# A sixth feature-major product pair and a new order of ScalarE's and VectorE's steps in a two-block sequence model

## What is computed

```python
    x = x + (p[i] @ ple_w[i]) * gate
    return rmsnorm(x, norm_final)
...
    h = rms_norm(x, norm_g[l])
    proj = jnp.einsum('bsd,de->bse', h, w_in[l])
    (a_q, a_k, a_v, a_z, m_q, m_k, m_v, m_o, m_z, m_i, m_f,
     c_a, c_b, c_z) = split_columns(proj)
    ...
    qk = jax.nn.silu(causal_depthwise_conv(jnp.concatenate([m_q, m_k], axis=-1), ...))
    ...
    u = c_a * jax.nn.sigmoid(c_b)
    u = causal_depthwise_conv(u, cv_dw_w[l], cv_dw_b[l])      # 31 taps
```

## Time and profile before

| | us |
|---|---|
| median of 3 runs (3367.03 to 3368.46) | 3367.67 |
| the profiled execution, its own time | 3364.18 |
| its span, first to last instruction | 3362.6 |
| PE busy | 3231.2 (96%) |
| DVE busy | 1950.9 (58%) |
| POOL busy | 1706.8 (51%) |
| ACT busy | 1240.3 (37%) |

### The profile page before, as it was taken

The page is one execution under the profiler, slowest core; times in us unless marked ns, Lnnn a source line. Parts: engine busy times, 40 slices in busy tenths (PEclk is TensorE's granted clock), DMA queues, the critical chain, the costliest instruction groups (busy, mean ns, idle before and its releaser), DMA issues. The chain is left out here.

```text
span 3362.6 us, 43705 instructions
## 1 busy us (share of the span) xinstructions
PE 3231.2 (96%) x16157; PEld 2632.0 (78%) x16157; DVE 1950.9 (58%) x2345; ACT 1240.3 (37%) x1871; POOL 1706.8 (51%) x1142
## 2 busy tenths in 40 slices
PE   5989999999999999999999999999999999898999
PEld 5767878888888778888878888888777788577887
DVE  8687355555555766793456555555758678355511
ACT  5323353333333443312343333333444312566511
POOL 5812856666666326542865556666523742244521
PEclk9999999999999999999999999999999999999999
DMA  6364111111111213323311111111212232425653
GB/s 233 115 132 133 51 52 56 50 50 50 54 52 50 94 44 125 119 101 134 113 60 48 53 50 50 50 54 52 94 48 103 94 122 99 178 79 181 209 149 105
DMA packets 156942, 309.90 MB, mean 92 GB/s; under 512 B 16752, under 2 KB 92016, under 8 KB 154112
## 3 DMA queue, kind: packets, MB, share of 16 engines
q1 hardware_dynamic: 140640, 265.88, 24.4%
q10 hardware_dynamic: 16160, 42.08, 3.3%
HBM read 234.98 MB, written 72.94 MB: 92 GB/s over the span
## 5 line engine op out<-in xcount | busy, mean ns | idle before, releaser
L2137 PE MATMUL ps_job<-AHL,WH 128*128 128x512 f32 x3072 | 951.6, 391 | 16.6 <-POOL WL L1531 10.0
L1531 POOL TENSOR_TENSOR WL<-WR,WH 128x1024 fp32r<-128x1024 f32 x170 | 427.0, 2512 | 770.8 <-ACT WH L1123 769.1
L2137 PEld LDWEIGHTS ps_job<-AHL,WH 128*128 128x128 f32 x3072 | 578.7, 189 | 141.2 <-POOL WL L1531 14.1
L2137 PE MATMUL ps_job<-AHL,WL 128*128 128x512 f32 x1536 | 599.8, 391 | 0.0
L1123 ACT CAST WH<-WR 128x1024 fp32r<-128x1024 f32 x214 | 225.0, 1052 | 752.7 <-PE ps_job L2137 509.3
L2137 PEld LDWEIGHTS ps_job<-AHL,WL 128*128 128x128 f32 x1536 | 289.8, 189 | 60.5
L1833 DVE SCALAR_TENSOR_TENSOR ps_job<-ps_job,RB 128x1024 f32<-128x1024 f32 (+1 forms) x80 | 79.9, 1017 | 405.6 <-PE ps_job L2137 396.1
L1592 POOL TENSOR_TENSOR OPS_L<-VS,OPS_H 128x1024 fp32r<-128x1024 f32 (+2 forms) x96 | 193.5, 2030 | 55.9 <-ACT OPS_H L1312 51.3
L2286 PE MATMUL ps_job<-OPS_H,WH 128*128 128x512 f32 x512 | 199.5, 390 | 0.7 <-POOL WL L1531 0.7
L2286 PE MATMUL ps_job<-OPS_L,WH 128*128 128x512 f32 x512 | 199.3, 389 | 0.0
L2286 PE MATMUL ps_job<-OPS_H,WL 128*128 128x512 f32 x512 | 199.3, 389 | 0.0
(11 more groups left out here) (535 smaller groups left out, 7209.3 us busy)
## 6 DMA issues: line engine op xcount, KB each, us to landing
WR<-in_wall SPq DMA_DIRECT2D x244, 512.0 KB, 3.3
fm_scratch<-VS ACTq DMA_DIRECT2D x32, 512.0 KB, 3.1
tm_scratch<-VS ACTq DMA_DIRECT2D x24, 512.0 KB, 2.7
s_Win<-in_x_chunk SPq DMA_DIRECT2D x8, 1024.0 KB, 7.9
s_U<-in_x_group SPq DMA_DIRECT2D x8, 1024.0 KB, 12.4
s_mt<-z_scratch SPq DMA_DIRECT2D x64, 128.0 KB, 4.6
prod_scratch<-s_Win SPq DMA_DIRECT2D x16, 512.0 KB, 2.6
X<-in_x_feat SPq DMA_DIRECT2D x2, 4096.0 KB, 15.8
```

Of the source, the lines that this page charges most:

```text
L1531: pool.tensor_tensor(dst, raw, src.bitcast(F32), ALU.subtract).then_inc(raw_free, 1)
L2137: last = pe.matmul(out, l, r, start=(k == 0 and i == 0), stop=(k == k_tiles - 1 and i == 2))
```

## The change

The pairs begin at j = 6, so that projections 6 and 7 (kind silu) become a pair as well. ScalarE, not VectorE, makes the scaled YR, after its activation of j == 1. VectorE makes the four sums at j == 1, ahead of the final rows. The casts and low parts of T move to j == 2 and 3. `third_sum` goes into the eviction of the odd job, ahead of its last tap or ahead of the plain eviction. The taps' counts after each j change.

```diff
-PAIRED_FM = range(8, 18, 2)
+PAIRED_FM = range(6, 18, 2)
...
-TAPS_AT = {j: 3 for j in range(18, 20)} | {j: 5 for j in range(20, 32)}
+TAPS_AT = {j: 3 for j in range(18, 20)} | {j: 2 for j in range(20, 24)} | {j: 4 for j in range(24, 28)} | {j: 8 for j in range(28, 32)}
...
                     take(j)
+                    if j == 1:
+                        act.wait_ge(xadd, N_XADD * tb + (2 + N_XADD))
+                        for k in range(KD):
+                            act.activation(YR[:, k], X[:, k], ACT.Copy, scale=gains[:, GAIN_OF[2], k:k + 1]).then_inc(f_raw, 1)
                     if j in (1, 2):
                         store_rows(j - 1)
-                    if j in (3, 4):
-                        t_high((range(KD // 2), range(KD // 2, KD))[j - 3], 1)
+                    if j in (2, 3):
+                        t_high((range(KD // 2), range(KD // 2, KD))[j - 2], 1)
...
+                def put(j):
+                    if KINDS[j] == "silu":
+                        take(j)
+                    store(j)
...
-                        store(j - 2)
+                        put(j - 2)
...
-                    store(j - 1)
+                    if i:
+                        put(j - 1)
+                    else:
+                        store(j - 1)
...
-                def convolve(j, i):
+                def convolve(j, i, between=None):
...
                         if k:
                             step(ins)
+                        if k == 1 and between:
+                            between()
...
-                def evict(j):
+                def evict(j, between=None):
                     if KINDS[j] == "conv":
-                        convolve(j, j - M_QK.start)
+                        convolve(j, j - M_QK.start, between)
                     else:
+                        if between:
+                            between()
                         slot_free(j)
-                        dve.tensor_tensor(V[j % 2][:], ps4[slot_of(j)][:], halves(RB[:]), ALU.mult).then_inc(copied, 1)
+                        done = scaled if KINDS[j] == "silu" else copied
+                        dve.tensor_tensor(V[j % 2][:], ps4[slot_of(j)][:], halves(RB[:]), ALU.mult).then_inc(done, 1)
...
                     if i:
-                        evict(j - 1)
-                    third_sum(n, FM, slots[1])
+                        evict(j - 1, lambda: third_sum(n, FM, slots[1]))
+                    else:
+                        third_sum(n, FM, slots[1])
...
                     if j == 1:
-                        for k in range(KD):
-                            dve.tensor_scalar(YR[:, k], X[:, k], gains[:, GAIN_OF[2], k:k + 1], None, ALU.mult).then_inc(f_raw, 1)
-                        final_rows()
-                    if j == 2:
                         dve.wait_ge(f_raw, KD * (tb + 1))
                         t_sums(1)
+                        final_rows()
                     if j == 3:
                         dve.wait_ge(st_x[1], 16 * tb + 16)
-                    if j == 4:
+                    if j == 3:
                         t_low(1)
```

## The result

| | us |
|---|---|
| after, median of 4 runs (3414.24 to 3418.81) | 3414.82 |
| before, same session, median of 4 runs (3365.11 to 3368.46) | 3367.35 |
| ratio, 95% interval | 1.0145, 1.0132 to 1.0159 |
| the profiled execution of after, its own time | 3415.3 |
| its span (before: 3362.6) | 3413.4 |

The change makes the kernel 1.4% slower. 3413.9 was forecast. The spans differ by 50.8 us, the medians by 47.5; the profiled execution of before was a quick one (3364.18 against a median of 3367.67), so the sum of 46.2 has to answer for 50.8, not for 47.5. About 3 us of the closeness of the forecast is luck.

What follows compares the result with a forecast made beforehand. TensorE, busy 96% of the span, was taken as the bound. Forecast: 40.0 us more at the fronts, less 5.5, 3.9 and 3.9, plus 19.5 for the tail: 46.2 more, 3367.7 + 46.2 = 3413.9 us; range 3392 to 3427.

Steps and rivals of the forecast that it cites:

- The queue at the front: ScalarE, each block: the first rows' store waits for the third final row, delaying tile 4's cast from 1263.06 to 1275.3.
- Tile 4's low part: GpSimd's subtraction ahead of job 4: shut out by VectorE's final rows, 7.7 us, ending at 1284.1 instead of 1271.9.
- the first wait: TensorE ahead of job 4 in each block: waits 10.8 us for GpSimd's subtraction of tile 4.
- a train with gaps: Rival: GpSimd gets in between final rows; eighth row and job 5 2.3 us later; 4.6 more, 3418.5; chance 0.15.
- Job 5: TensorE, each block: tile 5 stands behind T's low parts on GpSimd; starts at 1303.1, 18.9 us lost.
- The restart: TensorE runs at a lower granted clock after a long wait: 1.6 us lost, charged once a block.
- The tail: VectorE, block 1: 36 taps behind j = 27 take 51.8 us; TensorE waits 17.9 us inside j = 31.
- The small waits: Four TensorE waits on `third_sum` in block 1 and four at the gates in both blocks go: 3.9 us less each.

Runs made afterwards that it cites:

- b4: The kernel before, with VectorE waiting for its own last scaled row between the scalings and the final rows; 3364.77 us in one run.
- b1: The kernel before with only the change's new taps' counts added; 3381.88 us, ratio 1.0052 to before.
- a1: The kernel after with the taps' counts of before put back; 3400.06 us, ratio 1.0103 to before.
- b2: The kernel before with only `third_sum` put ahead of the last convolution step; 3359.67 us, ratio 0.9988 to before.
- the early stop: The kernel before, with VectorE waiting for its own scaled rows behind the fourth scaling instead of the eighth; 3366.63 us in one run.
- c1: The kernel after with stores behind the T_H casts, tile 5 ahead of T's low parts on GpSimd, and 21 taps behind j = 27; 3388.51 us, ratio 1.0063 to before.

## Why the prediction was right

**The queue at the front: right.** The store of the first rows went to stand behind the sums and final rows and held the cast of tile 4 back: forecast 1275.3, measured 1275.66. The run with the store moved shows that it is this.

**Tile 4's low part: wrong, and the sum hardly felt it.** The step "the overlap is now almost the same, so everything moves by the 12.2 us of the final rows", with 7.7 us for the subtraction, failed. The trace of after has 2.92, and the first wait is 5.76 us instead of 10.8. I took the 7.70 of before as what such a meeting costs. The same meeting in the kernel before costs 2.97 when VectorE pauses for 0.1 us ahead of the final rows (b4); in after, four sums that wait for one another stood ahead of them. The Trainium skill (SBUF — State Buffer, section SBUF: two separate sides: the shared pair of ports is held for the whole instruction, the other engine blocks until then) gave the right answer for after (2.92) and for the run with the stop (2.97). The train of before does not agree with it: GpSimd stood through the rest of a row, three more rows and a c_a step (7.70). The rival "a train with gaps" named what followed: the eighth row 2.1 us later (11.73 against 9.64), and job 5 with it.

**Job 5: right in mechanism, 1.4 us too small.** Predicted 18.9 us late, measured 1305.10 - (1251.95 + 3 x 10.94) = 20.3. The rival had 21.2. Five GpSimd steps and VectorE's four between them took 15.56 us, 16.0 were charged; they began at 1289.49 instead of 1287.1, of which 0.56 is the whole block's (its j = 2 began at 1251.95, not 1251.39) and the rest goes with the 2.1 above. The moved tile 5, with 12.6 us less in the fronts, shows that it was this order on GpSimd that cost.

**The restart: mis-sized.** 1.6 us were charged. Job 5 lost 12.59 - 10.94 = 1.65, right. In j = 31 it was more: from the use of the scans' sixth step to the next step of the same job (`m_ends`) are 8.7 us in after (2889.59 to 2898.28) and 5.9 in before (2845.04 to 2850.92), so 2.8. Behind the same wait b1 lost 2.2 and the run with tile 5 first 1.5, so one number doesn't fit them all. Job 4 lost 2.50, hidden behind job 5's wait, as said.

**The tail: right.** 51.8 us were charged for 36 taps and 17.9 for the wait; 51.58 and 17.73 came. b1 and a1 move the span by 16.8 and 16.6; 17.73 + 2.8 less what the four gate waits cost (4.6) is 15.9; the last 0.7 to 0.9 us are not placed.

**The small waits: right, and too small.** They go, as b2 (0.9988) and the gates of after and b1 show. 3.9 us were charged for each four; the stretches around them gave 5.7 and 4.6.

Put together in the spans: 2 x (20.3 + 1.65 - 0.5) = 42.9, less 5.5, 3.9 and 3.9, plus 20.5, is 50.1 of the 50.8; 46.2 were forecast. That it comes so near is luck in part. The two stretches from the first plain job to the gates are together 32.1 us longer in after, where this sum has 33.5 for them (42.9 less 5.5 and 3.9), the gates gave 4.6 and not 3.9, and the rest of the kernel ahead of the last stage 0.7. Against these stand 3.4 us lost from the first attention product to the end (463.2 us against 459.8), which the sum doesn't have. The change doesn't touch that stage, and the run with tile 5 first, which has all the rest of the change, takes 459.7 there; the cause stays open.

## What to carry to other kernels

When a step is moved on one engine, follow every queue in which something waits for it: here two stores, one row of casts and four low parts cost 43 us, where the fewer matmuls and waits were to give 14. Two waits of one chain are not two costs: find the one that ends last, and move that. And before an engine's slack in the middle of a kernel is spent, look for the point where it is due; the 15 more taps behind j = 27 came to 18 us of waiting at the scans.

## What was not expected of the hardware

A GpSimd subtraction of 2.4 us that comes while VectorE writes its final rows was let in behind the running row in after and in the run with the stop (2.92 and 2.97 us), and was kept out until that train was over in before and with the early stop (7.70), in both blocks of each kernel. A pause of 0.1 us (the final rows began 0.04 behind the scalings' end instead of 0.08 ahead of it), made by a wait of VectorE for its own last result, changed the one into the other. A pause ahead is no safe way in: among the taps of c1, four instructions behind a pause of 5.09 us, GpSimd was kept out for the seven taps, 10.52 us in all. For the end of this kernel the pause made no difference that one run could show (3364.77 us with the stop): either way the subtraction is in time there.

Each time it is let in, VectorE pays for it: eight final rows take 9.64 us with GpSimd kept out, 11.73 with one of its instructions among them, 16.09 with three (c1).
